# A two-block transformer layer in one program: the first decay exponentials, the key products and the last z unit in another order

## The reference, cut to what matters

```python
proj = h @ w_in[l]                       # 512 pool, 1024 z, 1536 xbc, 16 dt columns
y_pool = pool_mixer(proj[..., :s_z], pool_w[l], pool_b[l], pool_scale[l])
...
conv = jax.nn.silu(conv + conv_b)        # xs (1024), bs and cs (2 groups x 128 each)
dt = jax.nn.softplus(dt_raw + dt_bias);  A = -jnp.exp(a_log)
a_cs = jnp.cumsum(dt * A, axis=-1)
decay = jnp.exp(jnp.where(causal, a_cs[..., :, None] - a_cs[..., None, :], -jnp.inf))
cb = jnp.einsum("bclgn,bcsgn->bcgls", c, b)
y = jnp.einsum("bcgls,bgrcls,bcsgrp->bclgrp", cb, decay, xdt)      # + the state part
y = y + xs * d_skip
y = y * jax.nn.silu(z)                   # the gate
y_ssd = rmsnorm(y, ssd_norm)
...
y = jnp.concatenate([y_pool, y_ssd], axis=-1) @ w_out[l]
```

## Time and profile before

| | |
|---|---|
| median of three runs | 1382.64 us (1381.12 to 1383.38) |
| profiled execution, device time | 1384.36 us |
| its span in the profile | 1382.6 us |
| PE busy | 1350.9 us (98%) |
| DVE, ACT, POOL busy | 1009.5, 885.5, 651.4 us |
| chain that ended last | PE 76%, POOL 9%, issue 8%, DVE 4%, ACT 2% |

### The profile page before, as it was taken

How to read it: one execution, slowest core, us unless ns; L and a number is a source line. 1 busy time by engine, 2 the same in 40 slices (tenths; PEclk the granted TensorE clock), 3 DMA queues, 4 the chain that set the end, 5 groups by cost and what they waited for, 6 DMA issues and landing times.

```text
span 1382.6 us, 31396 instructions
## 1 busy us (share of the span) xinstructions
PE 1350.9 (98%) x9828; PEld 1254.0 (91%) x9828; DVE 1009.5 (73%) x2172; ACT 885.5 (64%) x1855; POOL 651.4 (47%) x499
## 2 busy tenths in 40 slices
PE   7999999999999999999999999999999999999997
PEld 4798999999999988999999999999988888888886
DVE  6678858888976696489990268888876666666665
ACT  5668765555445656547888687777765555555554
POOL 4896793000005867697999987777720000000000
PEclk9999999999999999999999999999999999999999
DMA  9776565999983643564555554444456656656652
GB/s 345 269 256 225 206 238 191 329 323 326 343 318 107 221 137 101 189 228 155 192 186 185 189 174 157 162 152 164 154 169 196 193 191 193 195 190 192 196 191 83
DMA packets 79287, 283.85 MB, mean 205 GB/s; under 512 B 8821, under 2 KB 8949, under 8 KB 79098
## 3 DMA queue, kind: packets, MB, share of 16 engines
q1 hardware_dynamic: 79226, 283.07, 59.9%
HBM read 281.99 MB, written 1.05 MB: 205 GB/s over the span
## 4 chain that ended last, share of the span: by engine, by line
PE 76%; POOL 9%; issue 8%; DVE 4%; ACT 2%; DMA 1%; POOLq 0%; SPq 0%; DVEq 0%; ACTq 0%
PE psA L1778 19%; PE psA L1782 18%; PE psA L1781 18%; POOL w_lo L564 9%; PE psD L1778 5%; PE psD L1781 5%; PE psD L1782 5%; PE psD L2237 1%; PE psD L2238 1%; DVE arena L1504 1%; ACT w_hi L621 1%; DMA xT<-x 1%; DVE arena L1511 0%; PE psA L1812 0%; DVE arena L1057 0%
## 5 line engine op out<-in xcount | busy, mean ns | idle before, releaser
L621 ACT CAST w_hi<-raw 128x512 fp32r<-128x512 f32 x864 | 530.0, 621 | 416.3 <-PE psA L1778 300.1
L564 POOL TENSOR_TENSOR w_lo<-raw,w_hi 128x512 fp32r<-128x512 f32 x476 | 633.9, 1353 | 344.0 <-ACT w_hi L621 338.4
L1778 PE MATMUL psA<-h_hi,w_hi 128*128 128x256 f32 x1568 | 448.7, 286 | 2.7 <-POOL w_lo L564 2.5
L1781 PE MATMUL psA<-h_lo,w_hi 128*128 128x256 f32 x1568 | 437.9, 279 | 0.0
L1782 PE MATMUL psA<-h_hi,w_lo 128*128 128x256 f32 x1568 | 437.2, 279 | 0.0
L1071 DVE TENSOR_TENSOR w_lo<-raw,w_hi 128x512 fp32r<-128x512 f32 x388 | 266.4, 692 | 152.2 <-ACT w_hi L621 151.1
L1778 PEld LDWEIGHTS psA<-h_hi,w_hi 128*128 128x128 f32 x1568 | 294.9, 188 | 6.7 <-POOL w_lo L564 3.1
L1781 PEld LDWEIGHTS psA<-h_lo,w_hi 128*128 128x128 f32 x1568 | 295.0, 188 | 0.1
L1782 PEld LDWEIGHTS psA<-h_hi,w_lo 128*128 128x128 f32 x1568 | 294.7, 188 | 0.0
L1778 PE MATMUL psA<-w_hi,u_hi 128*128 128x512 f32 x512 | 199.3, 389 | 0.5 <-DVE u_lo L1129 0.5
L1782 PE MATMUL psA<-w_hi,u_lo 128*128 128x512 f32 x512 | 199.2, 389 | 0.0
(11 more groups left out here) (386 smaller groups left out, 2106.8 us busy)
## 6 DMA issues: line engine op xcount, KB each, us to landing
raw<-expert_down SPq DMA_DIRECT2D x128, 512.0 KB, 3.2
raw<-expert_up SPq DMA_DIRECT2D x128, 512.0 KB, 4.3
arena<-ada SPq DMA_DIRECT2D x96, 512.0 KB, 5.2
raw<-gateup SPq DMA_DIRECT2D x44, 512.0 KB, 5.6
raw<-feat SPq DMA_DIRECT2D x28, 512.0 KB, 3.9
raw<-win SPq DMA_DIRECT2D x24, 512.0 KB, 3.3
raw<-down SPq DMA_DIRECT2D x22, 512.0 KB, 5.7
raw<-wout SPq DMA_DIRECT2D x20, 512.0 KB, 3.4
```

Of the source, the lines that this page charges most:

```text
L564: nc.gpsimd.tensor_tensor(w_lo[:, s * HALF:(s + 1) * HALF], raw_half(n), w_hi[:, s * HALF:(s + 1) * HALF].bitcast(F32), ALU.subtract).then ...
L621: nc.scalar.copy(w_hi[:, n % SLOTS * HALF:(n % SLOTS + 1) * HALF], raw_half(n)).then_inc(hi_ready, 1)
L1778: first = mm(o, w[0], m[0], start=start, stop=False, skip_group_check=True)
L1781: mm(o, w[0], m[1], start=False, stop=False, skip_group_check=True)
```

## The change

`cb` and the decay arguments of heads 0 and 1 are written among the twelve units on PE, the exponentials of heads 0 and 1 stand on ACT ahead of what belongs to the last z unit, DVE's copy of `cb` stands ahead of the window means, and its first weights stand ahead of the last pool group. The last z unit is copied out of PSUM, and its Silu is taken in place behind all exponentials, with a semaphore for the last `ssd_out`. The ring tables follow.

```diff
-          ... ("win2_z", 8), ("ssd_decay", 16), ...
+          ... ("win2_z", 7), ("first_decays", 2), ("win2_last", 1), ("ssd_decay", 14), ...
-          ("xs_tok", 4), ("pool", 4), ("cb", 2), ("ssd", 8), ...
+          ("xs_tok", 4), ("cb", 2), ("pool", 4), ("ssd", 8), ...
@@ ACT
-            for j in range(KC):
-                split(1)
-                A.free(nc.scalar.activation(z2T[:, Z2_Z + j, :], A.bank()[:, 0:T], ACT.Silu))
...
-            for h in range(SH):
...
+            z_last = z2T[:, Z2_Z + KC - 1, :]
+            for j in range(KC):
+                if j == KC - 1:
+                    act.wait_ge(d_drained, D_AT["dt_cols"] + 1)
+                    for h in range(2):
+                        decay_exp(h)
+                split(1)
+                if j == KC - 1:
+                    A.free(nc.scalar.copy(z_last, A.bank()[:, 0:T]))
+                else:
+                    A.free(nc.scalar.activation(z2T[:, Z2_Z + j, :], A.bank()[:, 0:T], ACT.Silu))
...
+            for h in range(2, SH):
+                decay_exp(h)
                 if h == 3:
                     act.wait_ge(d_drained, D_AT["pool"] + NPOOL)
                     upper_mix(NPOOL - 1)
+            act.wait_ge(a_drained, A_AT["win2_last"] + 1)
+            nc.scalar.activation(z_last, z_last, ACT.Silu).then_inc(sem("z_last"), 1)
@@ DVE
             for g in range(NPOOL):
                 pool_sums(g)
+            for g in range(SG):
+                Dr.free(V.tensor_copy(cbT[:, g, :], Dr.bank()[:, 0:3 * P]), settle=True)
             pool_means()
...
             for g in range(NPOOL):
+                if g == NPOOL - 1:
+                    ssd_weights(0)
                 Dr.free(V.tensor_scalar(mixT[:, g, :], ...))
                 if g >= 1:
                     lower_mix(g - 1)
-            for g in range(SG):
-                Dr.free(V.tensor_copy(cbT[:, g, :], Dr.bank()[:, 0:3 * P]), settle=True)
...
             def ssd_out(j):
+                if j == KC - 1:
+                    dve.wait_ge(sem("z_last"), 1)
@@ PE
-            behind = {0: (dt_cols,), ..., 8: (pooled, 0), 9: (pooled, 1), 10: (pooled, 2), 11: (pooled, 3)}
+            behind = {0: ((dt_cols,),), ...,
+                      5: ((cb, 0), (cb, 1)), 8: ((pooled, 0),), 9: ((pooled, 1),),
+                      10: ((pooled, 2), (ssd_decay, 0), (ssd_decay, 1)), 11: ((pooled, 3),)}
...
-            for h in range(2):
-                ssd_decay(h)
-            for g in range(SG):
-                cb(g)
```

More of the change, by code:

```diff
@@ L67 @@
 RING_A = (("tok_v", 4), ("gates", 1), ("mixers", 40), ("ssq2", 1), ("gate", 22),
-          ("ssq_both", 1), ("win2_pool", 4), ("win2_z", 8), ("ssd_decay", 16), ("x_scale", 1), ("ssq_ssd", 1), ("ssq_ffn", 1), ("query", 16),
+          ("ssq_both", 1), ("win2_pool", 4), ("win2_z", 7), ("first_decays", 2), ("win2_last", 1), ("ssd_decay", 14), ("x_scale", 1), ("ssq_ssd", 1), ("ssq_ffn", 1), ("query", 16),
           ("experts", 128), ("ssq_final", 1))
@@ L71 @@
           ("m_out", 4), ("ymT", 4), ("proj", 16), ("wout", 8), ("up", 22), ("down", 4), ("dt", 1), ("xbc", 12), ("dt_cols", 1),
-          ("xs_tok", 4), ("pool", 4), ("cb", 2), ("ssd", 8), ("wout2", 4), ("scores", 16), ("picksT", 4))
+          ("xs_tok", 4), ("cb", 2), ("pool", 4), ("ssd", 8), ("wout2", 4), ("scores", 16), ("picksT", 4))
 BANKS = 4
@@ L902, in _, with decay_exp @@
                     xbc_silu(XBC - 4 + j)
-            for j in range(KC):
-                split(1)
-                A.free(nc.scalar.activation(z2T[:, Z2_Z + j, :], A.bank()[:, 0:T], ACT.Silu))
[L906 to L910, removed]
-            for h in range(SH):
+            def decay_exp(h):
                 if h >= 4:
@@ L918, in _ @@
                                             bias=s_cols[:, 0, 1, h:h + 1]))
+            z_last = z2T[:, Z2_Z + KC - 1, :]
[9 more added lines that the diff above has]
+                    A.free(nc.scalar.activation(z2T[:, Z2_Z + j, :], A.bank()[:, 0:T], ACT.Silu))
+                if j >= KC - NPOOL + 1:
+                    act.wait_ge(d_drained, D_AT["pool"] + j - (KC - NPOOL))
+                    upper_mix(j - (KC - NPOOL + 1))
+            for h in range(2, SH):
+                decay_exp(h)
                 if h == 3:
@@ L1520, in _, with ssd_weights @@
                 pool_sums(g)
+            for g in range(SG):
+                Dr.free(V.tensor_copy(cbT[:, g, :], Dr.bank()[:, 0:3 * P]), settle=True)
             pool_means()
+            def ssd_weights(j):
+                g = j // (KC // SG)
+                dve.wait_ge(a_drained, A_AT["ssd_decay"] + 2 * j if j else A_AT["first_decays"] + 2)
+                w = ssd_w[:, j % 2 * 2:j % 2 * 2 + 2, :]
+                V.tensor_tensor(w, w, cbT[:, g, :].unsqueeze(1).broadcast_to([P, 2, 3 * P]),
+                                ALU.mult).then_inc(sem("ssd_w"), 1)
             for g in range(NPOOL):
+                if g == NPOOL - 1:
+                    ssd_weights(0)
                 Dr.free(V.tensor_scalar(mixT[:, g, :], Dr.bank()[:, 0:T], col("pool_b", g), col("pool_scale", g),
@@ L1545, in _ @@
             for j in range(KC):
-                ssd_weights(j)
                 if j >= 1:
+                    ssd_weights(j)
                     ssd_out(j - 1)
@@ L2136, in pooled @@
                            start=True, stop=True))
[L2138 to L2145, removed]
             def ssd_decay(h):
@@ L2152, in ssd_decay @@
                 A.full(mm(b[:, 0:3 * P], ident_r, mask_r, start=False, stop=True, skip_group_check=True))
+            behind = {0: ((dt_cols,),), 1: ((turn_xs, 0),), 2: ((turn_xs, 1),), 3: ((turn_xs, 2),), 4: ((turn_xs, 3),),
+                      5: ((cb, 0), (cb, 1)), 8: ((pooled, 0),), 9: ((pooled, 1),),
+                      10: ((pooled, 2), (ssd_decay, 0), (ssd_decay, 1)), 11: ((pooled, 3),)}
+            for j in range(NPOOL + KC):
+                unit(A, h_parts)
+                if j == NPOOL + KC - 2:
+                    pe.wait_ge(sem("decay_consts"), 7)
+                    pe.wait_ge(sem("u_lower"), 2)
+                for step, *which in behind.get(j, ()):
+                    step(*which)
+            stage_ends()
             def ssd_pair(j):
@@ L2165, in ssd_pair @@
                 Dr.full(last)
-            pe.wait_ge(sem("decay_consts"), 7)
-            pe.wait_ge(sem("u_lower"), 2)
-            for h in range(2):
-                ssd_decay(h)
-            for g in range(SG):
-                cb(g)
             for j in range(KC):
```

## The result

| | before | changed |
|---|---|---|
| median | 1383.12 us (20 runs, 1381.12 to 1384.68) | 1385.51 us (20 runs, 1383.01 to 1387.78) |
| profiled execution: device time, span | 1384.36, 1382.6 us | 1384.82, 1383.0 us |

The ratio is 1.0014, with a 95% interval of 1.0007 to 1.002 (the two medians alone, 2.4 us apart, give 1.0017): a slowdown that is measured, but that stays under the 0.2% that was set as the bound. Forecast was +0.14% and 1384.5.

What follows compares the result with a forecast made beforehand. PE, busy 98%, bounds the kernel; its restart hangs 8.87 us behind ACT's last exponential. Exponentials +0.2, table load 1.28, Silu 0.38 and hand-overs 0.04 make +1.9 on 1382.64: 1384.5 us, range 1383.5 to 1385.6 (8 in 10: 1382.5 to 1386.1).

Steps and rivals of the forecast that it cites:

- Copies of `cb`: DVE's two copies, 1.14 us, ahead of the means: end of the means unchanged, to +0.3; bound the full 1.14.
- Rival A: On DVE: the copies delay the means in full, 1.14 us; total +2.8, 1385.5 us; chance 0.17.
- First exponentials: On ACT and DVE: table load at about 506.2 us, first weights at 509.0 instead of 510.16.
- Second pair: On ACT and DVE: second weights start at 511.9 beside POOL's `w_lo`, third at 514.2 to 514.3; 1.2 us lead lost.
- The circle: Weights, pair, decay arguments and exponentials: unchanged, 7.82 us from 516.15 to the table load; exponentials end at +0.2.
- The late Silu: ACT's tail: table load 1.28, Silu 0.38 (bound 0.51), two hand-overs of 0.02 us, with nothing hiding them.
- the sign named: PE's restart follows ACT's squares at a distance of 7.47 us; if not, the forecast is wrong.
- Rival D: ACT's tail: its pipe empties at both loads, costing a second 1.28 us; +3.2, 1385.8 us; chance 0.05.
- PE full behind the restart: PE in the output projection: no holes from its restart on, so the +1.9 us there reaches the end.
- the sum: At PE's restart: +0.2 (exponentials) + 1.28 + 0.38 + 0.04 = +1.9 us; added to median 1382.64: 1384.5.
- Rivals B and C: B: front's 1.2 us lead kept, 1383.1 us, chance 0.12. C: ACT's new load hidden in a wait, 1381.8, chance 0.04.
- The chances: For the whole kernel's time: slower by over 0.2% 0.18, faster by over 0.2% 0.03, no change 0.79.

Runs made afterwards that it cites:

- the products alone: Kernel before with only the `cb` products moved behind PE's sixth unit and their copies ahead of the means: 1384.39 us against 1382.18, ratio 1.0018.
- Casts spread: Changed kernel with squares ahead of the root's table and the last z unit's two casts behind exponentials of heads 3 and 5: 1380.46 us, ratio 0.999.
- The tail alone: Kernel before with only the last z unit's Silu moved behind all exponentials: 1386.53 us against 1382.85, ratio 1.0024.
- the filled versions: Six matmuls of ones ahead of PE's wait for the sum of squares: 1383.49 us in the changed kernel, 1384.77 in the kernel before with only its Silu late.

## Why the prediction was right

- *Copies of `cb`.* The means end at 499.47 + 1.40 + 2.45 = 503.3, against 503.2 before: the copies cost 0.1. Before, one step of a mean met no POOL instruction (0.43); now two do (0.43 and 0.41 us), the one meeting less that was foreseen. Rival A's mechanism did not occur, neither here nor with the products alone.
- *First exponentials.* Table load at 506.15 on the old scale, forecast 506.2; first weights 508.83, forecast 509.0.
- *Second pair.* Start 511.76 and 1.39 us long, forecast 511.9 and about 1.4. The third weights came at 513.93 and not at 514.2 to 514.3: POOL's second `w_lo` ended at 512.34, as forecast (512.4), but the weights went on for only 0.74 behind it and `ssd_out(0)` took 0.85, where I had taken 0.9 for each. Casts spread shows that the casts and the meeting with POOL together took the lead. How much each took alone was not tried.
- *The circle.* It is as rigid as forecast, within 0.13: the third weights were 0.15 ahead, and the exponentials ended at -0.02, forecast +0.2.
- *The late Silu.* 1.28 and 0.42 (forecast 0.38), fully exposed: squares +1.71, restart +1.67. PE's restart follows the squares at 7.43 us, where 7.47 was the sign named. The tail alone has the same numbers. On the drain that the Trainium skill gives for each switch (ScalarE: Activation LUTs, What ACT_TABLE_LOAD costs: 1.38 us beside the load of 1.28), this trace does not agree: from the start of the new load to the squares it takes 3.13 us, and two loads, a Silu and the root's small instruction fill them. Rival D falls with it.
- *PE full behind the restart.* This step of the sum failed in size. The sum ended at the restart with +1.9 and took PE at full pace from there. The restart came at +1.67, and in the profiled execution 1.24 us more was lost behind it at the lower clock, a term that the sum put at nothing. So that the forecast of +0.14% equals the measured ratio is in part luck, two errors of opposite sign: 0.2 too much in the exponentials, and nothing for the slow stretch. In the traces +2.91 stands at the next reciprocal and in the medians +2.4, and against both the sum of 1.9 was too small.
- *Rivals B and C.* The lead was not kept; in casts spread, where its obstacle is taken away, 1.1 us of it is. No wait hid the tail.
- *The chances.* Half of A, D and a twentieth of the forecast add up to 0.17, not 0.18.

The median of before moved too, from 1382.64 over three runs to 1383.12 over twenty; that is part of why 1384.5 was 1 us below the measured 1385.51.

## What to carry to other kernels

Follow the chain of the stage to the next place where the bounding engine restarts, and look at what stands on it as a rigid string: a gain upstream of the string is capped by the engine's own arrival, a microsecond added on it is paid in full. A function that needs another table is cheapest where its engine waits anyway; squares need none of their own here, so the root's table could be loaded behind them. When a change lengthens a hole of TensorE, read the granted clock behind the hole as well, and see what filling it with matmuls of no use gives. Count from a landmark just ahead of the change: what ran before it differed by 2.45 us between the two traces here, about as much as the change costs.

## What the runs showed of the hardware that was not expected

- The clock fell to 0.50 for about 3.4 us at a hole with 1.57 and 0.57 us idle (and 0.67 us of work between) in the changed kernel, at one with 1.55 and 0.57 in the tail alone, and at one with 3.17 in the products alone. The fall came 0.4 us behind PE's restart, 0.4 us ahead of it, and 1.2 us behind the first pair. It did not come behind the 1.89 us ahead of the first pair in the kernel before, nor behind the 1.60 us ahead of the second in the changed one, nor behind the restart in the filled versions. A stretch of 3.4 us at half pace would cost 1.7; by the next reciprocal 1.24 of it was left.
- The slow stretch stands in both traces in which the squares wait for the Silu's and the root's load and the hole is left empty, and in neither of the two with the hole filled. Whether it comes in every execution is not shown.
- Two DVE copies out of PSUM took 1.15 us while POOL was at work in SBUF, without the delay that the means had beside it (1.40 instead of 0.43), and the weights with both inputs in SBUF took 1.39 instead of 0.96 beside a `w_lo`.
